# Blocks of 64 slots and one-run weights in the experts of a hierarchical MoE layer

## What is computed

```python
pg = softmax(xt @ w_rg + b_rg);  p_top, g_idx = top_k(pg, 1)          # 1 of 4 groups
v2, i2 = top_k(el_sel, 2)                                             # 2 of its 8 experts
gates = softmax(v2) * p_top;  expert_id = g_idx * 8 + i2
def run_block(xb, e):                                                 # rows of one expert
    h = silu(xb @ w_gate[e]) * (xb @ w_up[e])                         # 1024 -> 512
    return h @ w_down[e]                                              # 512 -> 1024
h = h + scatter_add(ys * slot_gate);  return rms_norm(h, final_g)
```

## Time and profile before

| | us |
|---|---|
| median of 3 runs | 2106.82 (2106.13 to 2109.68) |
| span of the profiled execution | 2107.0 |
| PE busy in it | 1993.2 (95%) |
| DVE, ACT, POOL busy | 1323.6, 1159.0, 846.2 |
| DMA bytes | 420.62 MB |

### The profile page before, as it was taken

The page is one execution under the profiler, slowest core; times in us unless marked ns, Lnnn a source line. Parts: engine busy times, 40 slices in busy tenths (PEclk is TensorE's granted clock), DMA queues, the critical chain, the costliest instruction groups (busy, mean ns, idle before and its releaser), DMA issues. The chain is left out here.

```text
span 2107.0 us, 39855 instructions
## 1 busy us (share of the span) xinstructions
PE 1993.2 (95%) x12627; PEld 1697.4 (81%) x12628; DVE 1323.6 (63%) x2411; ACT 1159.0 (55%) x2421; POOL 846.2 (40%) x1024
## 2 busy tenths in 40 slices
PE   7999999979999999989999689999999999999997
PEld 6888888867777787878788578888888888888886
DVE  5333333328888888845565568677777668695763
ACT  4211111128888889953333257666666657684662
POOL 3322222223656644431332345444444435444443
PEclk9999999989999999989999899999999999999998
DMA  7433333366363443224544579989999988998963
GB/s 227 136 120 120 122 121 120 112 171 165 105 166 105 126 114 91 69 70 154 168 158 140 204 242 357 355 276 307 302 283 318 339 266 277 361 347 271 310 200 88
DMA packets 320307, 420.62 MB, mean 200 GB/s; under 512 B 27289, under 2 KB 230681, under 8 KB 320192
## 3 DMA queue, kind: packets, MB, share of 16 engines
q1 hardware_dynamic: 290912, 351.34, 51.0%
q0 software_dynamic: 29296, 68.03, 12.5%
HBM read 344.35 MB, written 110.41 MB: 216 GB/s over the span
## 5 line engine op out<-in xcount | busy, mean ns | idle before, releaser
L742 ACT ACTIVATE prob<-score,nmax 128x512 f32<-128x512 f32 (+3 forms) x464 | 264.3, 579 | 24.9 <-DVE nmax L892 24.5
L60 PE MATMUL proj<-w_in_lo,n1T_hi 128*128 128x512 f32 (+1 forms) x640 | 244.1, 381 | 3.1 <-DVE w_in_lo L245 3.0
L62 PE MATMUL proj<-w_in_hi,n1T_hi 128*128 128x512 f32 (+1 forms) x640 | 239.5, 374 | 0.0
L61 PE MATMUL proj<-w_in_hi,n1T_lo 128*128 128x512 f32 (+1 forms) x640 | 239.4, 374 | 0.0
L892 DVE TENSOR_REDUCE nmax<-score 128x2 f32<-128x1024 f32 (+3 forms) x232 | 212.5, 919 | 41.5 <-PE score L940 39.8
L60 PE MATMUL u_ps<-wu_lo,xT_hi 128*128 128x256 f32 x752 | 216.3, 288 | 0.0
L61 PE MATMUL u_ps<-wu_hi,xT_lo 128*128 128x256 f32 x752 | 212.7, 283 | 0.0
L62 PE MATMUL u_ps<-wu_hi,xT_hi 128*128 128x256 f32 x752 | 212.6, 283 | 0.0
L1887 DVE TENSOR_TENSOR wg_lo<-raw_pieces,wg_hi 128x1024 fp32r<-128x1024 f32 x124 | 147.6, 1219 | 83.6 <-ACT wg_hi L1848 83.5
L807 POOL TENSOR_SCALAR prob<-prob,scale,lam 128x512 f32<-128x512 f32 (+3 forms) x168 | 137.7, 831 | 151.8 <-DVE scale L879 142.4
L264 DVE TENSOR_TENSOR cosx<-proj,rope_sb 128x512 f32<-128x512 f32 (+1 forms) x64 | 37.9, 592 | 219.3 <-PE proj L62 219.3
(11 more groups left out here) (261 smaller groups left out, 5210.4 us busy)
## 6 DMA issues: line engine op xcount, KB each, us to landing
raw_pieces<-in_w_down SPq DMA_DIRECT2D x64, 1024.0 KB, 12.0
raw_pieces<-in_w_gate SPq DMA_DIRECT2D x62, 1024.0 KB, 11.4
raw_pieces<-in_w_up SPq DMA_DIRECT2D x62, 1024.0 KB, 11.9
qk_scratch<-qkT SPq DMA_DIRECT2D x94, 256.0 KB, 2.6
xT_sb<-in_xT SPq DMA_DIRECT2D x16, 512.0 KB, 5.0
h<-in_x SPq DMA_DIRECT2D x16, 512.0 KB, 5.7
acc_scratch<-h SPq DMA_DIRECT2D x16, 512.0 KB, 3.0
n_scratch<-n SPq DMA_DIRECT2D x16, 512.0 KB, 4.9
```

The lines of the kernel that those rows point to most:

```text
L60: pe.matmul(out, hi, w_lo, start=first, stop=False)
L61: pe.matmul(out, lo, w_hi, start=False, stop=False)
L62: return pe.matmul(out, hi, w_hi, start=False, stop=last)
L742: act.activation(prob[:, n % RING, c, 0:w], score[:, n % BUFS, c, 0:w], ACT.Exp, bias=nmax[:, c, n:n + 1], accum_out=part[:, c, n:n + 1]). ...
```

## The change

An expert's first 128 tokens go into one full block (F, 128 slots), which now stands last, and the rest into small blocks (S) of 64 slots, ahead of it. With the counts above that is 15 small and 32 full blocks. A small block's rows sit on partitions 64 to 127 of the gathered x. Its stationary operand holds 64 high and 64 low columns (`xT_hi[:, k, 64:192]`, for which DVE copies the low part beside the high one after each `split_xT`), and a product takes two matmuls. Its result comes in two halves of the partitions which have to be added: ACT copies one half across (`y_part`), DVE adds. The host lays the weights out so that a pair is one run of 8 KB per partition. In both kinds of block `normalize(b)` moves behind `split_xT(b+1)` on DVE, in a full block `square(b)` moves behind `highs(3, 4, 5)` on ACT, and POOL's `store(b)` moves behind `move_on(b)` and the copy of `own`. POOL's slot list grows from 512 to 992 entries per partition.

```diff
 def source_pair(w_d, e, j):
-    gate, up, down = [w[bass.ds(e, 1), :, :].rearrange("o (k p) n -> p (o k) n", p=P) for w in w_d]
...
+    return w_d[j // 2][bass.ds(e, 1), :, j % 2 * 2 * PW:(j % 2 + 1) * 2 * PW].rearrange("o p n -> p (o n)")
...
             def expert(e, replaced):
...
+                first = small_count(eng, e)
+                last = small_count(eng, e + 1)
                 with eng.If(first < last):
-                    with eng.Fori(first, last) as b:
...
+                    with eng.Fori(first, last) as n:
+                        small_block(n + e, e, n, last - n)
+                full_block(last + e, e, replaced)
...
-                def one_block(b, e, replaced, here, after):
+                def one_block(b, here, after):
                     pool.wait_ge(x_in, b * 16 + 16)
                     pool.sem_inc(passed, 1)
                     gather(b + 1, within(after))
                     add(b)
-                    scale(b)
-                    store(b)
+                    normal_root(b)
+                    aim_store(b)
                     move_on(b)
                     pool.tensor_copy(own[:, :].bitcast(I32), slots[:, bass.ds(within(here), 1), :].bitcast(I32))\
                         .then_inc(own_ready, 1)
+                    store(b)
                     fetch_whole(b)
...
+                    smalls = small_count(pool, e + 2) - small_count(pool, e + 1)
+                    one_block(b, e, smalls * N_EXPERTS + (e + 1))
...
+                def small_block(b, e, n, left):
+                    act.copy(g_part[0:HP, :], g_ps[HP:P, :]).then_inc(part_out, 1)
+                    act.wait_ge(summed, n * 4 + 1)
+                    act.activation(hid[0:HP, :], hid[0:HP, :], ACT.Silu).then_inc(silu_ready, 1)
+                    copy_u_part(b, 0)
+                    copy_small_hT(b, 0)
+                    copy_u_part(b, 1)
+                    copy_xT(b + 1)
+                    copy_small_hT(b, 1)
+                    square(b)
+                    act.wait_ge(y_done, b + 1)
+                    act.wait_ge(own_ready, b + 2)
...
-                    highs(0)
-                    square(b)
-                    highs(1, 2)
+                    highs(0, 1, 2)
...
                     highs(3, 4, 5)
+                    square(b)
                     copy_hT(b, 0)
...
                 def split_xT(b):
...
+                    dve.wait_ge(xT_split, b + 1)
+                    dve.tensor_copy(xT_hi[:, :, P:], xT_lo[:, :, HP:]).then_inc(xT_packed, 1)
...
                     lows(0, 1, 2)
-                    normalize(b)
                     dve.wait_ge(silu_ready, b + 1)
...
                     split_xT(b + 1)
+                    normalize(b)
                     lows(6, 7, 8, 9, 10, 11)
...
+                def packed_product(out, packed, w_hi, w_lo, first, last):
+                    pe.matmul(out, packed, w_lo, start=first, stop=False)
+                    return pe.matmul(out, packed, w_hi, start=False, stop=last)
...
```

More of the change, by code:

```diff
@@ L1252, in block_table @@
                     dve.wait_ge(place_step, PLACED + 4)
[L1253 to L1256, removed]
+                    dve.tensor_copy(starts[0:1, :], start_row[:, :])
                 low_swa(0, 0)
@@ L1567, in source_piece @@
 def source_piece(w_d, e, k):
[L1568 removed]
+    return w_d[k // 4][bass.ds(e, 1), :, k % 4 * PW:(k % 4 + 1) * PW].rearrange("o p n -> p (o n)")
 def source_pair(w_d, e, j):
[L1573 to L1578 removed]
+    return w_d[j // 2][bass.ds(e, 1), :, j % 2 * 2 * PW:(j % 2 + 1) * 2 * PW].rearrange("o p n -> p (o n)")
 def raw_piece(raw, k):
@@ L1791, in _ @@
                 pool.memset(y[:, :], 0.0).then_inc(y_ready, 1)
+                pool.memset(hid[:, :], 0.0).then_inc(h_turned, 1)
+                first_smalls = small_count(pool, 1)
                 pool.wait_ge(own_free, 32)
-                gather(0, 0)
+                gather(0, within(first_smalls * N_EXPERTS))
                 pool.memset(whole[:, :], 0.0).then_inc(at_ready, 1)
@@ L1840, in copy_hT, with copy_small_hT, copy_u_part, small_block @@
                         .then_inc(hT_ready, 1)
-                def one_block(b, e, replaced, here, after):
+                def copy_small_hT(b, half):
+                    act.wait_ge(h_turned, b * 2 + (half + 2))
+                    src = g_ps if half == 0 else u_ps[:, 0, :]
+                    act.copy(hT_hi[:, 2 * half:2 * half + 2, HP:P],
+                             src[:, 0:HALF].rearrange("p (k n) -> p k n", k=2)[:, :, 0:HP]).then_inc(hT_ready, 1)
+                def copy_u_part(b, half):
+                    act.wait_ge(u_done, b * 2 + (half + 1))
+                    act.copy(u_part[0:HP, half, :], u_ps[HP:P, half, 0:HALF]).then_inc(part_out, 1)
+                def small_block(b, e, n, left):
+                    act.wait_ge(g_done, b + 1)
+                    act.wait_ge(h_turned, b * 2 + 1)
+                    act.wait_ge(y_ready, b + 1)
+                    act.copy(g_part[0:HP, :], g_ps[HP:P, :]).then_inc(part_out, 1)
[9 more added lines that the diff above has]
+                    act.wait_ge(own_ready, b + 2)
+                    act.activation(y[HP:P, :], y_ps[HP:P, :, :].rearrange("p a b -> p (a b)"), ACT.Copy,
+                                   scale=own[HP:P, 1:2]).then_inc(y_scaled, 1)
+                def full_block(b, e, replaced):
                     def highs(*ks):
```

169 lines of the change are left out of this document (123 added, 46 removed).

## The result

| | us |
|---|---|
| changed kernel, median of 4 runs | 2284.95 (2278.82 to 2287.72) |
| kernel before, beside it | 2108.25 (2106.13 to 2111.06) |
| ratio | 1.0836, 95% interval 1.0819 to 1.0853 |
| span of the profiled execution | 2285.6 |

The kernel got slower, as forecast, but by 177 us where 65 were predicted, and the time lies 45 us above the range. From the first to the last `turn_x`, the 46 steps take 2257.0 - 1241.0 = 1016.0 us instead of 845.8.

What follows compares the result with a forecast made beforehand. PE's own work was taken to bound all but 18 of the steps' 845.8 us. With the moved norm, 31 x 20.4 + 15 x 18.4 = 908 us, plus 2.5 at the start: 2107.0 + 65 = 2172 us, range 2090 to 2240.

Steps and rivals of the forecast that it cites:

- The moved norm as the deciding term: Norm behind split_xT(b+1) on DVE makes each turn_x wait through DVE, POOL and a DMA: 20.4 us per full block, 18.4 small.
- the loop: From turn_x through xT_lo, norm, store, whole and gather of x to a later turn_x, once per block: 20.4 us full.
- The short legs: From xT_lo's end to the gather's start: copy 0.5, final 1.3, store 2.4, whole 1.8, then 2.5 to the gather.
- The landing, 7.3 us: Gather of x from issue to arrival, a full block's leg with weights in flight: 7.3 us, 4.2 at the least.
- rival 1: Large weight packets delay the gather's landing further, 2.2 us per full block and 1.1 per small: 2257 us, chance 0.13.
- `turn_x` to `xT_lo`, 4.5 us: First leg in a full block, from turn_x's start to the end of xT_lo on DVE: 4.5 us.
- inside its own slack in the loop: PE at the lower clock after waiting in a small block would lose 5 us, most of it hidden by PE's slack.
- Small blocks on PE, 83 us saved: Two matmuls per product instead of three: 12.5 us against 18.0, 83 us for 15 blocks, where nothing else is late.
- Weights: Loads in 8 KB runs move no slower than 363 GB/s; at best all 18 us of waits for weights go.
- `own` with 3 us of cover: Later copy of own, which ACT's scaling of y awaits: ready 11 us after the gather's start, y at 14; no cost.
- DVE ahead of a small block: Small block's first sum stands behind the lows: PE waits 2 us for hidden rows, hidden if x comes later.
- the cost of the start: Longer slot list delays the first gather, between 0 and 5.0 us, taken as 2.5.

Runs made afterwards that it cites:

- 3: Kernel before with only the moved norm (normalize, square and store later), 128-slot blocks and old weight layout: 2154.0 us, ratio 1.0201.
- 10: Changed kernel with the norm early in full and small blocks, old weight layout, and store back ahead of move_on: 2093.1 us, ratio 0.9935 against the kernel before.
- 1: Changed kernel with only the weights' old layout back (runs of 1 to 4 KB): 2246.3 us, ratio 1.0638 against the kernel before.
- 5: Changed kernel with 30 transposes of the identity ahead of PE's wait for x in turn_x: 2274.2 us, ratio 1.0786 against the kernel before.
- 4: Kernel before with only the new weight layout, 8 KB per partition and pair: 2105.0 us, ratio 0.9971.
- 11: Kernel 10 with the weights in 8 KB runs instead of the old layout: 2147.4 us, ratio 1.0179 against the kernel before.
- 2: Changed kernel with normalize(b) moved ahead of lows(4, 5) in full blocks: 2214.0 us, ratio 1.0478 against the kernel before.

## Why the prediction was right in kind and wrong in size

- **The moved norm as the deciding term: right.** Alone it costs 41 us (3), with both norms early and the old layout the loss is gone (10), and the loop's legs stand in the chain.
- **The short legs: right.** In F to F, from the end of `xT_lo` to the gather's start it is 14.0 - 5.8 = 8.2 us; the terms 0.5, 1.3, 2.4, 1.8 and 2.5 make 8.5. The copy is 0.43. But the 2.5 us from `whole` to the gather were right by luck. They were put down to POOL beside the `lows`; beside the same `lows` the leg is 1.1 us in 3 and 1.3 in F to S. In F to F it is 2.2, with three loads of block counts where the others have one. Those loads had been priced at nothing, or 0.3 us.
- **The landing, 7.3 us: the term that failed first.** It was read at a gather issued 7.6 us after `turn_x`, beside 1 KB packets. In the loop the gather leaves at 13 to 14 and lands in 9.5: 16 x 2.2 + 15 x 2.3 + 15 x 0.2 = 73 us. With the old layout (1) some 30 us of it go: that is the packets' size, the mechanism of rival 1, which should have been part of the sum and no rival at 0.13, as rows 9 showed the turns. The other 43 us came with the later moment and what the gather meets there, for which the sum had no term. So rival 1's 2.2 us for full blocks, though the very number measured, fit by luck: its own cause is worth about half of them.
- **`turn_x` to `xT_lo`, 4.5 us: the other.** It was 5.8 and, in small blocks' steps, `final` came at 7.7 instead of 6.5: 16 x 1.3 + 15 x 1.25 + 15 x 1.2 = 58 us. I had the fall of the clock in mind and put it "inside its own slack in the loop". But `turn_x` is the first leg of the loop, and ahead of `xT_lo` DVE does `hT_lo`, which needs `turn_h(b, 1)` and so the first six matmuls of the down product. All of that runs at the clock after the wait (5: 1.05 us in F to F). The loop so feeds itself: longer wait, lower clock, longer loop. In 3, with waits of 2.7 us at most, it doesn't.
- The two make 131 us; 23 us come back, mostly at the gather's start in F-to-S steps (1.3 us after `whole`, and not 2.5). 131 - 23 = 108, and 2172 + 108 is within 6 us of 2285; the rest lies behind the last `turn_x` (28.6 us, 22.1 before).
- **Small blocks on PE, 83 us saved: not while the loop sets the pace.** The prediction said that this counts only where nothing else is late; in fact they cost 92 us with the norm late (1 against 3), and 0.65% of the time was won once both norms were early, with the old layout (10).
- **Weights: only in part.** No leg of the loop goes through a weight load, as said. But that 8 KB runs are worth up to 18 us failed: 4 gains some 6 us and shows no shorter steps, 11 shows 54 us of loss.
- **`own` with 3 us of cover: too much.** The prediction looked at ACT's scaling alone, and not at the store and `whole`, which stand behind `own` on POOL. In a full block `own` was 2 us ahead of `final`, and the loop behind it took over at once when the norm moved up (2). In all 15 steps behind a small block `own` ends 0.6 us behind `final`, since it follows POOL's root, which waits for ACT's `square`; so there the store waits for `own`, on the loop. ACT's own wait for it, up to 2.9 us, is off the loop.
- **DVE ahead of a small block: right.** PE waits 1.2 us there for the hidden rows, 17.5 us over 15 blocks, and x comes later anyhow. The first `turn_x` that counts came 1.9 us later (2.5 predicted), but it lies between 1238 and 1243 us over the runs with small blocks, so the cost of the start isn't shown.

## What to carry to other kernels

Moving an operation out of an engine's way can tie a queue that fetches ahead to the step that it fetches for; follow each wait on that queue round until it comes back to itself, and price every such loop, since the next one may be a microsecond or two behind. In a loop, take a DMA's landing at the moment and beside the traffic that the changed kernel will have, and PE's legs at the clock after its wait. Here small blocks paid only with the norm out of the loop for both kinds of block and with weights in small packets.

## What was unexpected of the hardware

- A gather of 128 rows of 4 KB lands in 4.2 to 4.5 us alone. Beside weights that are in flight all along it takes some 7.2 us in packets of 1 to 2 KB and 8.7 in packets of 8 KB at the early moment (kernel before, 4), and 8.5 beside packets of up to 4 KB and 9.5 beside 8 KB at the later one (1, changed kernel). The adding scatter of the same size goes from 9.9 to 11.9 us with 8 KB packets alone (4), and to 13 in the changed kernel.
- One contiguous run of 8 KB per partition shows as one packet of 8192 bytes. It made the weights' own landing faster (`w_up` 11.9 to 7.5 us on the median in 4) and the kernel hardly (0.3% in 4), or slower (1, 11).
- Behind a wait of 3.6 us PE came back at a granted clock of 0.56; with short transposes in the wait it was 1.00.
